# Cache attention of a hybrid decoder trunk: pages copied to a DRAM scratch and loaded as 32-feature tiles that VectorE turns, with sample rows loaded head by head

## What is computed

```python
def scores(c, kr):                      # c: latents of a page, kr: its rotary keys
    k = mla_keys(c, kr, w_kb, k_norm_g) # kn = c @ w_kb (8 heads x 128), k = rmsnorm([kn, kr])
    return einsum('bqhe,blhe->bhql', q, k) * scale
def page_step(carry, phys):             # phys = page_table[:, j], 16 pages a sequence
    c, kr = lat_pool[phys], rope_pool[phys]
    return update(carry, scores(c, kr), c)   # running softmax; acc += pr @ c
...
o_lat = acc / l
return einsum('bhqr,rhv->bqhv', o_lat, w_vb)
```

## Time and profile before

| | |
|---|---|
| median of 3 runs | 3094.15 us |
| profiled execution, span | 3093.2 us |
| TensorE clock granted, mean | 0.945 |
| cache attention, first layer | about 459 to 956 us |
| cache attention, second layer | about 1998 to 2493 us |
| GpSimd busy | 840.5 us (27%) |
| DMA packets | 471235, 281.94 MB |

### The profile page before, as it was taken

The page is one execution under the profiler, slowest core; times in us unless marked ns, Lnnn a source line. Parts: engine busy times, 40 slices in busy tenths (PEclk is TensorE's granted clock), DMA queues, the critical chain, the costliest instruction groups (busy, mean ns, idle before and its releaser), DMA issues. The chain is left out here.

```text
span 3093.2 us, 62907 instructions
## 1 busy us (share of the span) xinstructions
PE 2765.1 (89%) x24800; PEld 2537.1 (82%) x24800; DVE 1796.3 (58%) x3035; ACT 1354.4 (44%) x2174; POOL 840.5 (27%) x696
## 2 busy tenths in 40 slices
PE   7887779999997889899988867699999988898998
PEld 6876349999997779899977863499999886798998
DVE  4845454656655755499348453455565556554993
ACT  4733344445444343354356334344454443433542
POOL 0030000899990400000000300009999804000000
PEclk9999979999998989999989998799999989999999
DMA  5302102211115276465453021131211142764644
GB/s 132 101 5 81 46 15 75 63 50 54 35 35 177 71 197 166 106 163 139 119 123 84 4 80 46 26 92 39 57 43 39 54 157 78 204 164 109 163 134 119
DMA packets 471235, 281.94 MB, mean 91 GB/s; under 512 B 65294, under 2 KB 466489, under 8 KB 470315
## 3 DMA queue, kind: packets, MB, share of 16 engines
q1 hardware_dynamic: 468724, 276.85, 32.2%
q10 hardware_dynamic: 2232, 1.26, 0.2%
HBM read 258.75 MB, written 19.29 MB: 90 GB/s over the span
## 5 line engine op out<-in xcount | busy, mean ns | idle before, releaser
L1112 PE MATMUL key_banks<-w_kb_head,latent_T_head 128*128 128x352 f32 x1536 | 518.8, 338 | 0.0
L1112 PE MATMUL key_banks<-w_kb_rest,latent_T_head 128*128 128x352 f32 x1536 | 497.0, 324 | 0.0
L1112 PE MATMUL key_banks<-w_kb_head,latent_T_rest 128*128 128x352 f32 x1536 | 496.6, 323 | 0.0
L290 DVE TENSOR_TENSOR w_rests<-w_ring,w_heads 128x2048 fp32r<-128x2048 f32 (+1 forms) x152 | 326.3, 2149 | 163.9 <-ACT w_heads L284 163.7
L931 POOL TENSOR_TENSOR rwkv_state_tmp<-rwkv_state,vec 128x1024 f32<-128x1024 f32 x64 | 153.3, 2395 | 654.0 <-DMA rwkv_state<-in_state_rwkv_dram 649.1
L1257 DVE TENSOR_REDUCE w_kb<-key_sq 128x8 f32<-128x1024 f32 x256 | 309.3, 1208 | 0.0
L1172 ACT CAST latent_T_head<-turn_bank 128x256 fp32r<-128x256 f32 x256 | 95.5, 373 | 471.3 <-PE turn_bank L1090 298.5
L284 ACT CAST w_heads<-w_ring 128x2048 fp32r<-128x2048 f32 (+1 forms) x152 | 272.2, 1793 | 61.1 <-ACT conv_last_rows L1798 19.7
L1112 PEld LDWEIGHTS key_banks<-w_kb_rest,latent_T_head 128*128 128x128 f32 x1536 | 291.3, 190 | 0.0
L1112 PEld LDWEIGHTS key_banks<-w_kb_head,latent_T_head 128*128 128x128 f32 x1536 | 290.7, 189 | 0.0
L1112 PEld LDWEIGHTS key_banks<-w_kb_head,latent_T_rest 128*128 128x128 f32 x1536 | 290.0, 189 | 0.0
(11 more groups left out here) (567 smaller groups left out, 7140.1 us busy)
## 6 DMA issues: line engine op xcount, KB each, us to landing
w_ring<-in_ffn_w_up_dram SPq DMA_DIRECT2D x88, 512.0 KB, 4.9
latents<-in_cache_kv_latent_dram SPq DMA_DIRECT2D x256, 128.0 KB, 2.0
w_ring<-in_w_in_dram SPq DMA_DIRECT2D x52, 512.0 KB, 3.7
w_ring<-in_w_gate_dram SPq DMA_DIRECT2D x48, 512.0 KB, 3.9
w_ring<-in_w_in_dram SPq DMA_DIRECT2D x20, 1024.0 KB, 6.0
w_ring<-in_ffn_w_down_dram SPq DMA_DIRECT2D x32, 384.0 KB, 3.6
w_ring<-in_ffn_w_down_dram SPq DMA_DIRECT2D x32, 320.0 KB, 4.1
rope_keys<-in_cache_k_rope_dram SPq DMA_DIRECT2D x256, 32.0 KB, 1.8
```

The source lines that it names most:

```text
L290: ops.tensor_tensor(rests[:, slot, 0:tiles * P], ring[:, slot, 0:tiles * P], heads[:, slot, 0:tiles * P].bitcast(F32), ALU.subtract).then_ ...
L1112: last = nc.tensor.matmul(kbank[:, 3 * x + n, 0:KB], c[:, x, r * P:(r + 1) * P], w[:, r, cols], start=r == 0 and m == 0, stop=r == 1 and m ...
```

## The change

Four parts.

1. **Pages go through DRAM.** `gather_pages` copies each page, by its number, from the cache into scratch tensors `page_latents` and `page_ropes`, laid out so that position 4i+t of the page is row i, part t. Sequences 0 and 1 are copied in `mla_qkv`, sequence 2 in `mla_prompt`, sequences 3 to 7 in `cache_attention`, four pages in each step of SP's loop. The page table is loaded in `load_x`.
2. **Turning moves from TensorE to VectorE.** For four pages at a time, 8 DMAs load the page as 32-feature tiles, `latent_blocks` and `rope_blocks`, in runs of 32 floats (128 bytes), so that VectorE's transpose of 32x32 blocks gives the whole turned page: one STREAM_TRANSPOSE of 128x256 into `turn_bank` for each page and one of 128x128 into `kpT` for each two pages. It is done three pages ahead. The TensorE transposes are gone, and so is ScalarE's copy of `kpT`. The latents are loaded a second time, untransposed, for the value products.
3. **The copy of the scores (`taken`) moves** from VectorE to ScalarE.
4. **Sample rows head by head.** `mla_prompt` stores the rows with 6 DMAs ordered by head; `cache_attention` loads `vec` with one DMA and the state with 8, right after the first four pages; `ssd_project` stores `vec_y` with one DMA in place of 8.

```diff
+def gather_pages(sp, k, b, pages, gathered):
+    for j in pages:
+        page = sp.value_load(k.pages[0:1, ds(b * PAGES + j, 1)], min_val=0, max_val=NPOOL - 1)
+        row = ds(page, 1)
+        sp.dma_start(k.d["page_latents"][b:b + 1, :, j, :].rearrange("o i c -> (o i) c"),
+                     k.ldram("cache_kv_latent")[row].rearrange("o (i t) r -> (o i) (t r)", t=4)).then_inc(gathered, 16)
+        sp.dma_start(k.d["page_ropes"][b:b + 1, :, j // 2, :, j % 2, :].rearrange("o i t c -> (o i) t c"),
+                     k.ldram("cache_k_rope")[row].rearrange("o (i t) c -> (o i) t c", t=4)).then_inc(gathered, 16)
...
@@ mla_qkv, sync
                 sp.dma_start(w_q[:, :, :], ...).then_inc(loaded, 16)
+                n = sum(gather_pages(sp, k, b, range(PAGES), gathered) for b in range(2))
+                sp.wait_ge(gathered, n)
@@ mla_prompt, sync
+                copied = gather_pages(sp, k, 2, range(PAGES), gathered)
                 sp.wait_ge(row_kept, 12)
-                sp.dma_start(k.d["scratch_vec"].rearrange("t n d -> t n d"), rows[:, :, :]).then_inc(rows_out, 16)
-                sp.wait_ge(rows_out, 16)
+                for n in range(6):
+                    sp.dma_start(k.vec_rows[n].rearrange("h r d -> r h d"),
+                                 rows[:, n, :].rearrange("r (h d) -> r h d", d=64)).then_inc(rows_out, 16)
+                sp.wait_ge(rows_out, 96)
+                sp.wait_ge(gathered, copied)
@@ cache_attention, sync
+                def load_blocks(n):
+                    b, g, i = n // 4, n % 4, n % BLK          # BLK = 3
+                    if n >= BLK:
+                        sp.wait_ge(turned, 4 * (n - BLK + 1))
+                    if b >= 3 and g == 0:
+                        sp.wait_ge(gathered[b], 32 * PAGES)
+                    latents = k.d["page_latents"][b][:, 4 * g:4 * g + 4, :].rearrange("i j (m q f) -> q i (j m) f", q=4, f=32)
+                    ropes = k.d["page_ropes"][b][:, 2 * g:2 * g + 2, :, :, :].rearrange("i j t x (h f) -> x h i (j t) f", f=32)
+                    for q in range(4):
+                        rows = slice(32 * q, 32 * q + 32)
+                        sp.dma_start(blk[rows, i, :, :, :, :].rearrange("i j t r f -> i (j t r) f"), latents[q]).then_inc(in_b[i], 16)
+                        sp.dma_start(rblk[rows, i, :, :, :].rearrange("i j t f -> i (j t) f"), ropes[q // 2, q % 2]).then_inc(in_b[i], 16)
...
-                for slot in range(2):
-                    for g in range(4):
-                        load(slot, slot, g)
-                for b in range(NB):
-                    for n in range(6):
-                        sp.dma_start(k.vec[16 * b:16 * b + 16, n, :, :], ...).then_inc(rows_back, 16)
-                sp.dma_start(k.state[:, :, :], ...).then_inc(rows_back, 16)
+                load_blocks(0)
+                sp.dma_start(k.vec[...], k.vec_rows.rearrange("n h (b t) d -> (h b) n (t d)", b=NB)).then_inc(rows_back, 16)
+                for b in range(NB):
+                    sp.dma_start(k.state[b:P:NB, :, :]..., k.ldram("state_rwkv")[b:b + 1]...).then_inc(rows_back, 16)
+                load_blocks(1)
+                load_blocks(2)
+                for half in range(2):
+                    load_ropes(0, half)       # 4 DMAs each
+                    load_latents(0, half)     # 4 DMAs each
+                for b in range(NB):
+                    for g in range(4):
+                        n = 4 * b + BLK + g
+                        if n < 4 * NB:
+                            load_blocks(n)
+                        if b + 3 < NB:
+                            gather_pages(sp, k, b + 3, range(4 * g, 4 * g + 4), gathered[b + 3])
+                        if g >= 2 and b + 1 < NB:
+                            load_latents(b + 1, g - 2)
+                            load_ropes(b + 1, g - 2)
@@ cache_attention, tensor
-                        if j + 1 < PAGES:
-                            turn(b, slot, uses, j + 1)
...
@@ cache_attention, scalar
-                    last = nc.scalar.copy(ch[:, x, :], xbank[:, 0:2 * P])
-                    if x == 0:
-                        last = nc.scalar.copy(kpT[:, j // 2 % 2, :], xbank[:, 2 * P:3 * P])
+                    nc.scalar.copy(ch[:, x, :], xbank[:, :]).then_inc(headed, 1)
...
+                        nc.scalar.copy(s[:, slot, j, :], kbank[:, bank, o:o + 32]).then_inc(taken, 1)
@@ cache_attention, vector
+                def turn(n):
+                    x, group, at = n % 2, n // 4, n % 4
+                    i = group % BLK
+                    if at == 0:
+                        dve.wait_ge(in_b[i], (group // BLK + 1) * 128)
+                    if x == 0:
+                        if n >= 4:
+                            dve.wait_ge(scored, n - 2)
+                        nc.vector.transpose(kpT[:, n // 2 % 2, :], rblk[:, i, at // 2, :, :]...)
+                    if n:
+                        dve.wait_ge(t_kept, n)
+                    nc.vector.transpose(xbank[:, :]..., blk[:, i, at, :, :, :]...).then_inc(turned, 1)
...
+                        if base + j + AHEAD < NB * PAGES:     # AHEAD = 3
+                            turn(base + j + AHEAD)
                         dve.wait_ge(squared, base + (j + 1))
-                        nc.vector.tensor_copy(s[:, slot, j, :], kbank[:, bank, o:o + 32]).then_inc(taken, 1)
@@ ssd_project, sync
-                        for b in range(NB):
-                            sp.dma_start(k.d["scratch_y"]..., k.vec_y[16 * b:16 * b + 16, :, :]).then_inc(y_out, 16)
+                        sp.dma_start(k.y_by_head.rearrange("h (b t) d -> (h b) t d", b=NB), k.vec_y[:, :, :]).then_inc(y_out, 16)
```

More of the change, by code:

```diff
@@ L975, in cache_attention @@
     GROUPS = len(VALUES)
+    BLK = 3
+    AHEAD = 3
     KEEP, FOLD, DIVIDE = 13, 14, 15
@@ L1002, in cache_attention @@
         kbank = st.ps("key_banks", [P, 6, BANK])
-        xbank = st.ps("turn_bank", [P, BANK])
+        xbank = st.ps("turn_bank", [P, 2 * P])
         mbank = st.ps("misc_bank", [P, BANK])
-        in_l = [[st.sem(f"latents_loaded{i}_{g}") for g in range(4)] for i in range(2)]
+        in_l = [[st.sem(f"latents_loaded{i}_{h}") for h in range(2)] for i in range(2)]
+        in_r = [st.sem(f"rope_keys_loaded{h}") for h in range(2)]
+        in_b = [st.sem(f"blocks_loaded{i}") for i in range(BLK)]
+        gathered = {b: st.sem(f"pages_gathered{b}") for b in range(3, NB)}
         w_heads, w_split, q_headed, q_split = (st.sem(n) for n in (
@@ L1047, in _ @@
             def _(sp):
[L1048 to L1053, removed]
@@ new lines, in load_latents, with load_ropes @@
+                def load_latents(b, half):
+                    if b >= 2:
+                        sp.wait_ge(outed, (b - 2) * GROUPS + half + 1)
+                    for t in range(4):
+                        sp.dma_start(lat[32 * t:32 * t + 32, b % 2, 8 * half:8 * half + 8, 0:KVRANK],
+                                     k.d["page_latents"][b][:, 8 * half:8 * half + 8, t * KVRANK:(t + 1) * KVRANK]).then_inc(in_l[b % 2][half], 16)
+                def load_ropes(b, half):
+                    if b >= 1:
+                        sp.wait_ge(rope_sq, (b - 1) * 2 + half + 1)
+                    for t in range(4):
+                        sp.dma_start(kpe[32 * t:32 * t + 32, half, :, :].rearrange("i (j x) c -> i j (x c)", x=2),
+                                     k.d["page_ropes"][b][:, 4 * half:4 * half + 4, t, :, :].rearrange("i j x c -> i j (x c)")).then_inc(in_r[half], 16)
@@ L1079, in _ @@
             def _(pe):
[L1080 to L1089, removed]
-                        nc.tensor.transpose(xbank[:, 2 * P:3 * P], pair, k.col("ident")).then_inc(turned, 1)
-                    else:
-                        last.then_inc(turned, 1)
                 def body(b, slot, uses):
@@ L1099, in body @@
                         pe.wait_ge(t_kept, base + (j + 1))
-                        if j + 1 < PAGES:
-                            turn(b, slot, uses, j + 1)
-                        elif not is_last(b):
-                            turn(b + 1, 1 - slot, uses + slot, 0)
                         if not (is_first(b) and j < 2):
@@ L1131, in finish @@
                             pe.wait_ge(exped, b + 1)
+                        for half in range(2):
+                            if VALUES[at][0] == 8 * half:
+                                pe.wait_ge(in_l[slot][half], b // 2 * 64 + 64)
                         for j in range(*VALUES[at]):
```

62 lines of the change are left out of this document (34 added, 28 removed).

## The result

| | before | after |
|---|---|---|
| median | 3093.4 us (4 runs) | 3168.5 us (4 runs, 3165.47 to 3169.32) |
| profiled span | 3093.2 us | 3166.7 us |

A forecast was written before the change was run, and what follows sets the result against it. TensorE was taken to bound cache attention. Per layer 38.4 us saved on pages minus 2 for longer waits, over two layers 73 us, took 3094 to 3021 us; range 3006 to 3085.

The forecast's parts named there:

- SP's list: SP's issuing in cache attention: 51.5 us a sequence with gather against TensorE's 53; cost 0, with thin cover.
- third rival: SP bounds cache attention at 0.6 us a block DMA and 1.9 a gathered page: 3069 us; chance 0.09.
- The prediction's own signs of being wrong: TensorE under 95% busy between first and last key, or an earlier stage ending later; SP without pauses means third rival.
- The page: TensorE's keys in cache attention: removing transposes saves 0.30 us a page, 38.4 us a layer; bounds 43 and 23.
- The spread wait: TensorE's 0.46 us wait at the spread of the maxima: 7 such waits grow by about 0.3, 2 us a layer.
- VectorE: VectorE in cache attention: busy 318 us in a stage of some 425, 75%, not the bound.
- first rival: GpSimd stretches VectorE's transposes in cache attention, so VectorE bounds it: 3076 us, about 3060 with half; chance 0.12.
- The 128-byte packets: Block loads in cache attention: 15 ns a packet, 4.8 us of every DMA engine for four pages; bounds 8 and 31.
- second rival: Block DMAs bound cache attention: past TensorE's time at 31 ns a packet, 3210 us at 40 ns; chance 0.14.
- The stage's DMA share: DMA engines in cache attention: 9 us for four pages against TensorE's about 13.3; fits, at 68%.
- Start and other stages: Keys start 2 us earlier, page 4 about 2 us late, net 0; other stages 0, or 3 a layer.
- GpSimd: GpSimd (POOL) in cache attention: starts near 476, ends about 860 and stays hidden, cost 0.

The follow-up runs named there:

- the second experiment: Changed kernel without any copy in cache attention: sequences 3 to 7 read the pages of sequences 0 to 2 again; 3040.51 us, ratio 0.9821.
- the fixed copies: Changed kernel with each step's four gathered pages in cache attention replaced by three DMAs of the same bytes from a fixed place; 3040.43 us, ratio 0.9821.
- the kernel with blocks first: Kernel with gathers early, with second and third blocks loaded before sample rows and state, and 40 instead of 48 pages gathered in rwkv_tiles; 3033.37 us, ratio 0.9802.
- gathers early: Changed kernel with most gathers moved to earlier stages (48 pages in rwkv_tiles), and 28 left in cache attention, two a step; 3046.02 us, ratio 0.9848.
- the score copy on VectorE: Kernel with gathers early, with the score copy moved back from ScalarE to VectorE; 3062.5 us, ratio 0.9892.

## Why the prediction was wrong

**SP's list: the step that failed.** It said 51.5 us a sequence and "Cost 0, but with thin cover". It is 66.3. Of the 14.8 us:

- The gathered page takes 2.12, not 1.72: 16 x 0.4 = 6.4 us. The 1.72 of the earlier trace rows holds two issues of 0.33, which are loads into SBUF. Copies within DRAM issue in 0.50 and 0.55 us, 0.39 more for the two. The instruction was the same, the direction and the shape of the transfer were not, and so the row did not price it. Which of the two matters no run isolates.
- The 32 block DMAs go by in 0.49 and 0.61, 0.55 on average, not 0.50: 1.6 us.
- The remaining 6.8 us are for the most part (5.5, by the 25 us in 540 to 840 us) issues that take 0.9 to 1.8 us in place of 0.45 to 0.56, above all the blocks right behind the second load of the latents (685.31 to 687.51 above). They go with the copies' traffic: without copies such issues cost SP 5 us in 300 in place of 27, as the second experiment shows, and no term of the prediction stood for that. I read them as SP waiting for the DMA queues to take more; the trace shows their length, not what holds them.

The third rival (chance 0.09) named this mechanism, but at 0.6 and 1.9 us a DMA and a page, so 59 us a sequence, and hence 3069, still faster than before. With 66.2, five sequences in each of two layers lose (66.2 - 53.7) x 10 = 125 us against TensorE's pace; the fixed copies gave back 128. The sum turned sign because 12.5 us of wait by far exceed the 4.3 us that a sequence saves (58.0 us between first scores before, 53.7 at TensorE's pace now). A margin of 1.5 us in 53 should have been carried as the main risk, not priced at nothing. The prediction's own signs of being wrong came true: TensorE is busy 445 of 497 us between the first key and the last score, 90% where it wanted 95%; SP's list has hardly a pause; and `mla_prompt` ends later than before.

**The page.** I forecast 0.30 us saved; it is 0.24. After, in steady state (the kernel with blocks first):

```profile
651.19 0.30 PE L1158 MATMUL key_banks<-qr,w_kb 128*128 128x32 f32 x2
651.33 0.41 PE L1154 MATMUL key_banks<-w_kb_head,latent_T_head 128*128 128x352 f32 x1
651.57 0.32 PE L1154 MATMUL key_banks<-w_kb_rest,latent_T_head 128*128 128x352 f32 x1
...
654.28 0.30 PE L1158 MATMUL key_banks<-qr,w_kb 128*128 128x32 f32 x2
```

Score to score is 3.09, against 3.33 before. The first key steps by 0.24, the others by 0.16. It did so before too. There the first key stood between two lines of the earlier trace rows, 0.24 ahead of the second (704.27):

```profile
704.03 0.41 PE L1112 MATMUL key_banks<-w_kb_head,latent_T_head 128*128 128x352 f32 x1
```

So the 18 keys take 17 x 0.16 + 0.24, and I had counted that 0.08 as part of the transposes.

**The spread wait** was to grow by 2 us a layer. It shrank: with gathers early the same wait totals 7.0 us in both layers, where it had been 17.9. With the score copy on VectorE it is 12.1, so a good part of it is that copy. From the first score of the first stage to the last, 455.8 us before became 422.4 with blocks first: 33.4 a layer for the page and the wait together, against 36.4.

**VectorE** was right: 318 us forecast for the piece of the earlier trace rows, and 309 there in the changed kernel, 315 in the one with blocks first. The first rival (GpSimd in the way) is false: both transpositions hold their length while GpSimd works (ns min/median/max; estimated 420 and 270 ns).

```profile
L1287 DVE STREAM_TRANSPOSE turn_bank<-latent_blocks x256: 410/440/461, 475.1 to 2536.3; 128x256 f32<-128x256 f32 x128
```

```profile
L1284 DVE STREAM_TRANSPOSE w_kb<-rope_blocks x128: 296/302/315, 474.8 to 2533.1; 128x128 f32<-128x128 f32 x128
```

**The 128-byte packets** were right, and the second rival false. Over 885 to 897 us only block loads run (packets, MB, share of 16 engines):

```profile
q1 hardware_dynamic: 3962, 0.49, 26.7%
```

0.267 x 16 x 12 us / 3962 = 13 ns a packet, against 15 taken and 31 needed for the rival. The Trainium skill (DMA: Bandwidth & Descriptors, Specifications) wants 512 bytes or more in a transfer for the full rate, and names a read-modify-write below that. The packets here agree with it in part: for its bytes the 128-byte packet is dear, 13 ns where a quarter of the 31 ns of 512 bytes is 8, while the 256-byte one of the earlier trace rows is not, 15 ns against a half. The stage's DMA share was to be 68% at TensorE's pace; it is 81% in the window of the fastest kernel above, where TensorE is busy 53.90 of 54 us. It still fits.

**Start and other stages.** "Net 0" at the start was wrong. The keys do start 2 us earlier, as forecast: 8.3 us behind the stage's first load in both layers, against 10.3 before. But page 4 of the first sequence lies 9.6 and 7.9 us behind page 3 in place of 3.1, so the late block costs 6.5 and 4.8 us where I had 2. The kernel with blocks first took that back. In `mla_prompt`, SP was at its gathers when the rows were ready:

```profile
442.26 0.55 SPq L320 DMA_DIRECT2D page_ropes<-in_cache_k_rope_dram  x1
442.85 3.64 SPq L729 DMA_DIRECT2D scratch_vec<-sample_rows  x6
```

The store went out at 442.85 and not at 433.09; the stage is 4 us longer in the first layer and 2 in the second, where I had 0, or 3 with dearer gathers. It also slows the stage behind it, `mla_absorb`, of which the change takes nothing but the load of the page table. TensorE's first matmuls there, before and after:

```profile
442.42 1.94 PE L848 MATMUL absorb_banks<-const,w_kb 128*128 128x128 f32 x16 [1.10 <-PEq L228]
```

```profile
449.40 3.38 PE L866 MATMUL absorb_banks<-const,w_kb 128*128 128x128 f32 x16 [4.44 <-PEq L228]
```

TensorE stood idle for 4.44 us in place of 1.10, the granted clock over the stage was 0.70 in place of 0.80 (first layer), and the stage took 1.7 and 2.2 us more in the two layers. With 12 gathers in `mla_prompt` in place of 16, TensorE's part of it is back at the length of before (16.2 us in the first layer). So the forecast misses the 3040 of the kernel with fixed copies by 19 us, even with SP's list out of the way. By stages, that kernel's cache attention is 30.6 and 29.1 us shorter than before and not 36.4 (page, spread and start), `mla_prompt` 3.2 and 2.4 longer, and `mla_absorb` 2.8 and 2.1 longer. That makes 24 us; the other stages gave some 4 back, and I have no cause for that.

**GpSimd** was right: it starts at 487.65, ends at 869, and stays hidden.

## What to carry over

When work moves from loads on demand to many small DMAs, count the issuing queue as an engine: every DMA, register read and wait in its list, in us for each period of the loop, beside the engine that sets the pace. Price a DMA by a row of the same direction and shape, since the 0.33 us of a load here was 0.50 and more for a copy or a tile load; do not call a 3% margin free, and leave room for issues that grow beside other traffic (some 6 us of 66 here). Put the slow part of the list into stages where the queue is idle, and measure what it costs there. A late transfer is found by following an in-order list back: TensorE's wait named ScalarE, ScalarE's VectorE, and VectorE's the DMA.

## What the chip showed that I had not expected

- DMA issue on SP depends on the transfer: 0.33 us for a page into SBUF, 0.45 and 0.56 for the block loads, 0.50 and 0.55 for copies within DRAM, and up to 2.1 in 540 to 840 us of the changed kernel, mostly for blocks (33 of the 39 issues over 0.7 us). A register read with its address work adds 0.7 us (2.12 against 1.43).
- After the 6-us stall shown above, the granted clock was 0.50 in 632.9 to 637.4 us, the level of 1.2 GHz, with keys at a step of 0.29 us in place of 0.16, and 1.00 again from 638.1:

```profile
632.90:637.40 4.50, 4.50 (x16) 4.50 (x16) 2.43 (x5) 0.62 (x2) 3.95 (x8) 0.50 0.46 128
638.10:650.00 11.90, 10.90 (x80) 10.20 (x80) 5.20 (x11) 5.37 (x12) 11.51 (x6) 1.00 0.90 146
```

  So this stall cost TensorE some 2 us more (15 x 0.13). Here SP's pace hid it; in `mla_absorb`, above, nothing hid it.
- A packet of 128 bytes took 13 ns on a DMA engine, about as long as one of 256 bytes (15 ns) and less than half of the 31 ns of 512 bytes.
